# Expert tables of a decoder step: own buffer for one tile's weighed coefficients, an earlier dot activation, and other places for loads and weighings

## The reference, cut to what matters

```python
u = jnp.take(u_tab, eidx, axis=0)
act = jax.nn.gelu(jnp.einsum('nd,nhkd->nhk', xb, u).astype(jnp.float32), approximate=False)
coef = (gates * act).astype(xb.dtype)
return jnp.einsum('nhk,nhkd->nd', coef, jnp.take(v_tab, eidx, axis=0))
```

## Time and profile before

| | |
|---|---|
| median of 3 runs | 4967.91 us (4966.55 to 4977.75) |
| profiled execution, its own time | 4966.24 us |
| its span in the trace | 4964.5 us |
| PE busy | 4578.4 us (92%) |
| DVE busy | 3089.5 us (62%) |
| ACT busy | 1163.1 us (23%) |
| POOL busy | 2185.8 us (44%) |

### The profile page before, as it was taken

The page is one execution under the profiler, slowest core; times in us unless marked ns, Lnnn a source line. Parts: engine busy times, 40 slices in busy tenths (PEclk is TensorE's granted clock), DMA queues, the critical chain, the costliest instruction groups (busy, mean ns, idle before and its releaser), DMA issues. The chain is left out here.

```text
span 4964.5 us, 76173 instructions
## 1 busy us (share of the span) xinstructions
PE 4578.4 (92%) x29021; PEld 4413.5 (89%) x29021; DVE 3089.5 (62%) x5466; ACT 1163.1 (23%) x2078; POOL 2185.8 (44%) x1486
## 2 busy tenths in 40 slices
PE   8999999999989989998999788879989998998998
PEld 6999999899778879997999788878888898988987
DVE  4225630210267662444898888868888888888887
ACT  3112321111233330032222333321211212122122
POOL 0233333232033212341555577755655655556563
PEclk9999999999999989998999888989999999999999
DMA  5122222343431214442221488888888998988986
GB/s 184 52 60 81 94 99 86 104 122 116 140 99 46 54 36 151 139 130 82 83 81 67 161 288 289 303 303 305 309 306 294 313 309 297 316 292 304 311 307 232
DMA packets 572716, 911.53 MB, mean 184 GB/s; under 512 B 150088, under 2 KB 397896, under 8 KB 570629
## 3 DMA queue, kind: packets, MB, share of 16 engines
q1 hardware_dynamic: 424192, 422.36, 26.6%
q0 software_dynamic: 111744, 406.90, 23.7%
q10 hardware_dynamic: 36640, 80.36, 4.5%
HBM read 775.67 MB, written 133.84 MB: 183 GB/s over the span
## 5 line engine op out<-in xcount | busy, mean ns | idle before, releaser
L2601 PE MATMUL ea_banks<-h_high,ea_uT_high 128*128 128x336 f32 x2048 | 676.6, 330 | 83.7 <-ACT ea_coef L3507 62.0
L2601 PE MATMUL ea_banks<-h_high,ea_uT_low 128*128 128x336 f32 x2048 | 666.7, 326 | 0.0
L2601 PE MATMUL ea_banks<-h_low,ea_uT_high 128*128 128x336 f32 x2048 | 664.1, 324 | 0.0
L121 PE MATMUL p_in<-h_high,w_in_high 128*128 128x352 f32 x1536 | 495.5, 323 | 0.0
L121 PE MATMUL p_in<-h_low,w_in_high 128*128 128x352 f32 x1536 | 492.3, 320 | 0.0
L121 PE MATMUL p_in<-h_high,w_in_low 128*128 128x352 f32 x1536 | 491.8, 320 | 0.0
L2601 PEld LDWEIGHTS ea_banks<-h_high,ea_uT_high 128*128 128x128 f32 x2048 | 402.8, 197 | 93.5 <-ACT ea_coef L3507 68.1
L2576 POOL DMA_INDIRECT yT<-in_peer_u,gt_index x278 | 363.5, 1308 | 233.7 <-DVE h_low_plain L3619 114.3
L2576 POOL DMA_INDIRECT ea_u_raw<-in_peer_v,gt_index x192 | 269.1, 1402 | 311.2 <-DVE h_low_plain L3619 270.8
L2601 PEld LDWEIGHTS ea_banks<-h_low,ea_uT_high 128*128 128x128 f32 x2048 | 402.0, 196 | 0.0
L2601 PEld LDWEIGHTS ea_banks<-h_high,ea_uT_low 128*128 128x128 f32 x2048 | 400.3, 195 | 0.0
(11 more groups left out here) (525 smaller groups left out, 11802.8 us busy)
## 6 DMA issues: line engine op xcount, KB each, us to landing
w_in_raw<-in_w_in SPq DMA_DIRECT2D x88, 512.0 KB, 3.8
ex_gate<-tmp_gates SPq DMA_DIRECT2D x64, 672.0 KB
ea_u_raw<-in_peer_uT SPq DMA_DIRECT2D x66, 512.0 KB, 3.3
w_mb_raw<-in_peer_v SPq DMA_DIRECT2D x64, 512.0 KB
ea_uT_low_plain<-in_peer_uT SPq DMA_DIRECT2D x62, 512.0 KB
ex_lv_low_plain<-in_peer_v SPq DMA_DIRECT2D x62, 512.0 KB
tmp_acts<-ea_coef ACTq DMA_DIRECT2D x64, 336.0 KB
tmp_gates<-yT SPq DMA_DIRECT2D x7, 3072.0 KB, 11.6
```

The costliest lines, as they stand in the source:

```text
L121: last = pe.matmul(banks[0:rows, n, 0:CH], a[:, kk, 0:rows], b[:, kk, chunk(n)], start=(kk == 0 and a is wt.high[s] and b is high), stop=( ...
L2601: last = pe.matmul(acts.banks[:, n, 0:CD], a[:, c, :], b[:, c, dense(n)], start=(c == 0 and a is acts.uT_high[s] and b is high), stop=(c = ...
```

## The change

- A new buffer `weighed0`. `weigh_live(g, 0)` writes there instead of in place; `round_live` and `cut_live` of tile 0 read it. Tile 1 stays in place. The wait in `gelu(g, 0)` becomes one for the weighing of the turn before; that of `gelu(g, 1)` is unchanged.
- In ACT's list `raise_dots(g)` stands ahead of `raise_live_u(g + 1, 1)`.
- In SP's list the two `load_v(g + 1, s)` stand behind the next stash tiles' `load_gates`, not ahead of `load_live_u(g + 1, 1)`.
- In DVE's list `weigh_stash(g + 1, 0)` stands behind `sum_up(g, 3)` instead of `sum_up(g, 4)`, and three rows are taken ahead of a sum or weighing instead of behind it, so that the last two rows of a turn alone stand behind `sum_up(g, 7)`, as before, and none between `weigh_stash(g + 1, 1)` and it.

```diff
--- before.py
+++ after.py
@@ -3263,6 +3263,7 @@
 
         gate = sb("gate", [P, ND // GATE_BLOCK, 2, GATE_BLOCK])
         kept = sb("kept", [P, ND])
+        weighed = [sb("weighed0", [P, ND])[:, :], acts.coef[:, 1, :]]
         s_high, s_low, l_high, l_low = ([sb(f"{n}{s}", [P, ND], F32R) for s in range(2)] for n in ("s_high", "s_low", "l_high", "l_low"))
         v_raw = wt.raw
         lv_high = [sb(f"lv_high{s}", [P, KT, P], F32R) for s in range(2)]
@@ -3345,11 +3346,11 @@
                     load_live_u(g + 1, 0)
                 load_gates(live(g, 0), (s_low_made, 2 * g + 2))
                 if not last:
-                    for s in range(2):
-                        load_v(g + 1, s)
                     load_live_u(g + 1, 1)
                     load_kept(g + 1, 0, 2 * g + 2)
                     load_gates(2 * g + 2, (l_weighed, 2 * g + 2))
+                    for s in range(2):
+                        load_v(g + 1, s)
                     load_kept(g + 1, 1, 2 * g + 3)
                     for s in range(2):
                         load_live_v(g, s, lv_plain, lv_in, (multiplied, KT * (g + 1)))
@@ -3484,7 +3485,7 @@
                 act.wait_ge(l_weighed, 2 * g + s + 1)
                 if s == 0:
                     act.wait_ge(multiplied, KT * (g + 1))
-                act.copy(l_high[s][:, :], acts.coef[:, s, :]).then_inc(l_high_made, 1)
+                act.copy(l_high[s][:, :], weighed[s]).then_inc(l_high_made, 1)
 
             def round_stash(g, s):
 
@@ -3502,8 +3503,10 @@
             def gelu(g, s, first=False):
                 for n in range(DC):
                     act.wait_ge(acts.chunk_done, first_chunk(g, s) + n + 1)
-                    if n == 0 and not first:
-                        act.wait_ge(l_low_made, 2 * (g - 1) + s + 1)
+                    if n == 0 and s == 0 and not first:
+                        act.wait_ge(l_weighed, 2 * (g - 1) + 1)
+                    if n == 0 and s == 1 and not first:
+                        act.wait_ge(l_low_made, 2 * g)
                     act.activation(acts.coef[:, s, part_of(n)], acts.banks[:, n, 0:CD], ACT.Gelu).then_inc(acts.chunk_kept, 1)
 
             def raise_live_u(g, s):
@@ -3533,9 +3536,9 @@
                 if not last:
                     raise_live_u(g + 1, 0)
                 gelu(g, 1, first)
+                raise_dots(g)
                 if not last:
                     raise_live_u(g + 1, 1)
-                raise_dots(g)
 
             def finish(size, squares, of, t):
                 act.activation(squares, of, ACT.Square, accum_out=out_total[0:size, t:t + 1]).then_inc(out_squared, 1)
@@ -3574,7 +3577,7 @@
             def weigh_live(g, s):
                 dve.wait_ge(gate_in, 16 * (2 * g + 1) + 16)
                 dve.wait_ge(acts.chunk_kept, first_chunk(g, s) + DC)
-                dve.tensor_tensor(by_blocks(acts.coef[:, s, :]), by_blocks(acts.coef[:, s, :]), gate[:, :, s, :], ALU.mult).then_inc(l_weighed, 1)
+                dve.tensor_tensor(by_blocks(weighed[s]), by_blocks(acts.coef[:, s, :]), gate[:, :, s, :], ALU.mult).then_inc(l_weighed, 1)
 
             def cut_stash(g, s):
                 dve.wait_ge(s_high_made, 2 * g + s + 1)
@@ -3582,7 +3585,7 @@
 
             def cut_live(g, s):
                 dve.wait_ge(l_high_made, 2 * g + s + 1)
-                dve.tensor_tensor(l_low[s][:, :], acts.coef[:, s, :], l_high[s][:, :].bitcast(F32), ALU.subtract).then_inc(l_low_made, 1)
+                dve.tensor_tensor(l_low[s][:, :], weighed[s], l_high[s][:, :].bitcast(F32), ALU.subtract).then_inc(l_low_made, 1)
 
             def cut_v(g, s):
                 dve.wait_ge(v_high_made, 2 * g + s + 1)
@@ -3662,17 +3665,16 @@
                     cut_live_u(g + 1, 1)
                 take_rows(g, v + 2, v + 4)
                 sum_up(g, 3)
+                if not last:
+                    weigh_stash(g + 1, 0)
                 take_rows(g, v + 4, v + 6)
                 sum_up(g, 4)
-                if not last:
-                    weigh_stash(g + 1, 0)
-                take_rows(g, v + 6, v + 7)
+                take_rows(g, v + 6, v + 8)
                 sum_up(g, 5)
-                take_rows(g, v + 7, v + 9)
+                take_rows(g, v + 8, v + 10)
                 sum_up(g, 6)
                 if not last:
                     weigh_stash(g + 1, 1)
-                take_rows(g, v + 9, v + 10)
                 sum_up(g, 7)
                 take_rows(g, v + 10, ROWS)
```

## The result

The changed kernel takes 4807.31 us in the median of 4 runs (4804.64 to 4825.19), the kernel before 4969.6 us (4 runs, 4966.55 to 4977.75). The ratio is 0.9669, with a 95% interval of 0.9651 to 0.9688. Forecast were 4834 us and a range of 4765 to 4900. The profiled execution has a span of 4806.9 us.

The account below looks back on a forecast made before the run. DVE was taken as the bound: 43.2 us of work, 3.54 for rows and 0.3 for moved loads make 47.04 us a turn, 4.38 less than 51.42; over 30 turns, plus 3 us, this gives 4834 us, range 4765 to 4900.

Parts of the forecast that it names:

- DVE is the chain; a turn is 43.2 us plus its waits: Experts stage: DVE idles only for gathered rows, coefficients and kept values, 8.15 us of a 51.42 us turn.
- The buffer is worth nothing by itself: PE's 1.9 us gap at `gelu` goes, but the stall only moves to `cut_live_v`, so no gain alone.
- The coefficients' wait goes: `raise_dots` ahead of the second `raise_live_u` on ACT ends before DVE needs it: gain 2.92 us a turn.
- The kept wait goes: Six rows and three sums between the two weighings cover the kept load: 1.69 us a turn go.
- Loads moved; all covers are positive, 0.3 us: Later-requested stash gates, values and kept load land in time, rows 13 to 17 too; 0.3 us a turn allowed.
- Rows 6 and 7: DVE's wait for these gathered rows, 106.2 us in 30 turns, 3.54 a turn, was left unchanged.
- DVE stays the bound by a hair: At a changed turn's last sum DVE arrives 0.5 us after PE, whose floor is 44.5 us a turn.
- The first rival: Row 7's wait goes with the values and PE becomes the bound: 44.9 us a turn, 4770 us, chance 0.12.
- POOL as the bound: Rival: 20 gathers a turn, slowed by the port shared with DVE, take 48.0 us: 4863 us, chance 0.08.

Follow-up runs that it names:

- the two orders alone: The kernel before with only SyncE's and VectorE's order changed, no buffer, `raise_dots` in its old place: ratio 0.9672.
- `cut_stash` early: Both `cut_stash` put ahead of both `cut_v` and two dots: in the changed kernel 0.9575; in the kernel before with only SyncE's and VectorE's order changed 0.9580.
- without live gates: The changed kernel without the load of the live tiles' gates, which are weighed with what lies in the buffer: 4760.09 us, ratio 0.9565.

## Why the prediction was right, point by point

- **DVE is the chain; a turn is 43.2 us plus its waits.** Right, and the step that carried the most. It holds to 0.1 us after the change and sized what came off.
- **The buffer is worth nothing by itself.** Right: 1.0006 alone, 0.9674 without it. The stall moved to `cut_stash`, not to `cut_live_v` as I wrote.
- **The coefficients' wait goes, 2.92 us a turn, by the place of `raise_dots`.** The size was right, the credit wrong. The wait has two sufficient cures. With SyncE's order the live tile lands in time and the place of `raise_dots` does nothing (0.9678 without it); without that order it gives 2.2 of the 2.9 us. The sum counted the wait once, so the total did not suffer.
- **The kept wait goes, 1.69 us a turn.** Right as a wait, wrong as a gain that can be added on its own: alone nearly all of it came back (P 51.19 against 51.42).
- **Loads moved; all covers are positive, 0.3 us.** Two were: values and kept load are never waited for. The stash gates too. The failure is the sentence that the live tile's gates are requested at D + 9 "as before, and the landing relative to D does not move", and that no cover was worked out for them. The request did not move (D + 9.05). DVE's arrival did: free for them at D + 20.8 to 22.0 before, with less waiting ahead at rows 6 and 7 it now comes as early as D + 17.6. The landing stayed at its median (the last packet ends at D + 17.9 in both kernels) but spread out: at the latest D + 21.4 before, D + 23.8 now. The 15 short turns have 10.0 of the 33.2 us, by the early arrival. The others have 23.2, most of it where the gates landed late, as in the long turn above, where DVE could begin only at D + 24.0. This wait, 0.7 us in all 30 turns before and left out of the earlier trace rows, measured 1.11 us a turn against the 0.3 allowed.
- **Rows 6 and 7: "I leave this wait as it is", 3.54 us a turn.** This is the term that was mis-sized: all rows together measured 1.59 us, the dots' rows alone 0.82. I had put the wait down to what moves beside these rows in SyncE's queue. In the short turns the same loads stand there and the rows hardly wait. Shown is that the wait comes with the gather of 4.41 us at the head of POOL's chain, that this gather comes when DVE did not stop for PE at its last sum, and that both go when the wait for gates goes. Why the stop makes the gather short is not shown.
- **DVE stays the bound by a hair, PE's floor is 44.5 us a turn.** The floor is 44.75. In half of the turns the hair was on the other side. The first rival, PE as the bound, is what those turns are; the other half is the forecast. The sum, 43.2 + 3.54 + 0.3 = 47.04, became 43.2 + 1.59 + 1.11 + 0.36 = 46.26, which over 30 turns is 23 of the 27 us between 4834 and 4807. That the total came so near is in part luck: the rows gave 1.95 us a turn more than forecast, and the gates and PE took 1.17 of it back.
- **POOL as the bound.** Did not come. The Trainium skill, "SBUF — State Buffer", "Who interferes with whom", would have gathers slowed as DVE's waits close. POOL's busy time went from 932.18 us in 30 turns to 893.10, although DVE's share rose from 84 to 93%. So the trace does not show that cost. It does not refute the port either, since fewer long gathers may outweigh it. The reading that a gather takes 0.94 us while DVE is idle was too narrow: that at 4025.80 in the trace of before took 0.94 us too, and DVE did not stop in it.

## What to carry to other kernels

When the work and the waits of one engine add up exactly to the time, its waits are still not independent gains: removing one brings the engine early to the next load, so alone it may give nothing (0.9988) and together with another order of requests 1.3%. After pricing the waits that go, list every later load of that engine that was just covered, in order, with how much earlier the engine will now arrive and with the latest landing of all turns, not that of one; the one with the smallest cover is the next bound. The remedy here was an earlier request, by moving the last reader of its buffer. An edit that freed an engine off the chain (the buffer) was worth nothing here, although it closed a gap of 1.9 us a turn in the trace.

## What the runs showed that I had not expected

The loop has two kinds of turn that tend to follow themselves. In one a gather takes 1.75 us and the turn 44.75; in the other the gather of the same row, starting at the same 0.84 us before the same DVE instruction, takes 4.41, the rows behind it mostly come late, and the turn lasts 46 us and more. Fewer long gathers go with less time, though not strictly. Between 3340 and 4720 there are 25 to 28 in the kernel before, each single edit and the changed kernel without VectorE's order (P 48.87 to 52.08), 20 with the two orders alone (46.90), 18 without SyncE's order (48.11), 17 without the buffer (46.50), 11 in the changed one (46.25), 10 without the dots' place (46.13), 4 and 2 with `cut_stash` early (45.24 and 45.05), none without live gates (44.76).

DVE's instructions around the gather are the same in both kinds, so it is not their kind alone that makes it long. The bytes that move in its first us do not tell them apart either: 201 to 414 KB in the short ones of the changed kernel, 295 to 430 KB in the long ones. What does is whether DVE had stopped for PE at the last sum, some 2.3 us earlier. With such a stop the whole phase of PE and ACT against DVE is fixed too (the mark stands 3.36 us behind PE's first product), so which of the two it is, the stop or the phase, was not separated.

The granted clock rose from 0.96 to 0.99 though no edit is aimed at it. Two gaps of PE, of 1.51 and 2.26 us, stood in nearly every turn before; in the short turns now there is none. The clock fell to its lower level 31 times in the 30 turns before and 8 times in those after.
